# A hybrid decoder step: two small products of the cached attention get the full 128x128 shape, and the memory scores of a block stand in one place

## The reference, cut to what matters

```python
def mem_attend(q, mem_k, mem_v):                       # prompt: 256 memory tokens, 4 heads of width 64
    s = jnp.einsum('bshd,bmhd->bhsm', qh, mem_k).astype(jnp.float32) * (HEAD_DIM ** -0.5)
    pr = jax.nn.softmax(s, axis=-1).astype(q.dtype)
    return jnp.einsum('bhsm,bmhd->bshd', pr, mem_v).reshape(B, S, MEM_W)

def attend(q_lat, q_rope, ckv_new, krope_new):         # sample: one token against its paged cache
    s_past = jnp.einsum('bqhr,bkr->bhqk', q_lat, ckv_past) + jnp.einsum('bqhd,bkd->bhqk', q_rope, krope_past)
    ...
    pr = jax.nn.softmax(s, axis=-1).astype(ckv_new.dtype)
```

## Time and profile before

| | |
|---|---|
| median of 3 runs | 3482.54 us |
| span of the profiled execution | 3478.6 us |
| time outside the span, against the median | 3.9 us |
| TensorE busy | 3399.5 us (98%) |
| TensorE on the chain that ended last | 88% |
| VectorE, ScalarE, GpSimd busy | 58%, 36%, 7% |
| mean granted TensorE clock | 0.997 |
| TensorE idle before L827, for ScalarE's `Sm` | 4.5 us, 12 times |

### The profile page before, as it was taken

One profiled execution on the slowest core, in us unless ns is written; L12 is line 12 of the kernel. 1 busy time (PEld: TensorE's weight loads), 2 busy tenths in 40 slices (PEclk: granted clock), 3 DMA queues, 4 the chain that ended last, 5 costly groups with the idle time before them and its releaser, 6 DMA issues.

```text
span 3478.6 us, 80470 instructions
## 1 busy us (share of the span) xinstructions
PE 3399.5 (98%) x33076; PEld 2589.1 (74%) x33076; DVE 2030.8 (58%) x5212; ACT 1264.2 (36%) x3599; POOL 243.5 (7%) x284
## 2 busy tenths in 40 slices
PE   7999999999999999999999999999999999999998
PEld 6778686877869778686567787869777687776864
DVE  4656565665656556565346566666656565564653
ACT  2333334242343423524433233333423435234343
POOL 4100100000010000000041001000000000000000
PEclk9999999999999999999999999999999999999999
DMA  8654453626336163252366635436173351732512
GB/s 234 206 175 151 158 178 119 204 75 201 130 115 208 52 211 120 106 186 70 111 200 190 206 125 179 157 126 208 52 236 119 124 176 50 244 104 96 192 56 69
DMA packets 281024, 514.82 MB, mean 148 GB/s; under 512 B 30037, under 2 KB 215571, under 8 KB 268115
## 3 DMA queue, kind: packets, MB, share of 16 engines
q1 hardware_dynamic: 258903, 463.96, 40.7%
q0 software_dynamic: 11648, 41.95, 3.5%
q10 hardware_dynamic: 10108, 3.76, 0.4%
HBM read 473.15 MB, written 47.49 MB: 150 GB/s over the span
## 4 chain that ended last, share of the span: by engine, by line
PE 88%; ACT 4%; DVE 3%; issue 2%; DMA 2%; DVEq 1%; POOL 0%; ACTq 0%; POOLq 0%; SPq 0%
PE bank L823 81%; PE bank L827 7%; DMA win<-in_w_in 1%; DVEq L1555 1%; DMA wout<-in_w_out 1%; ACT Q L2603 1%; ACT PT L2718 1%; ACT qr L2602 0%; DVE mix L1785 0%; ACT Sm L2673 0%; ACT Q L2601 0%; DVE swaa L1783 0%; DVE mix L1781 0%; ACT hT L2426 0%; ACT PT L2523 0%
## 5 line engine op out<-in xcount | busy, mean ns | idle before, releaser
L823 PE MATMUL bank<-hT,win 128*128 128x256 f32 (+3 forms) x6384 | 1190.7, 339 | 6.5 <-DMA win<-in_w_in 3.3
L823 PEld LDWEIGHTS bank<-hT,win 128*128 128x128 f32 (+1 forms) x6384 | 951.1, 186 | 145.0 <-issue 33.4
L823 PE MATMUL bank<-wout,win 128*128 128x128 f32 x3136 | 379.9, 276 | 0.0
L823 PEld LDWEIGHTS bank<-wout,win 128*128 128x128 f32 x3136 | 364.6, 192 | 1.0
L823 PE MATMUL bank<-kv,Q 96*128 96x512 f32 (+3 forms) x640 | 276.4, 529 | 0.2
L1922 DVE TENSOR_REDUCE ml<-bank 128x1 f32<-128x512 f32 (+3 forms) x320 | 195.2, 610 | 124.5 <-PE bank L823 114.1
L827 PEld LDWEIGHTS bank<-cst,Sm 128*128 128x128 f32 x1344 | 157.5, 140 | 134.9 <-issue 72.0
L2673 ACT ACTIVATE Sm<-bank,ml 128x512 f32<-128x512 f32 (+3 forms) x320 | 199.8, 625 | 76.8 <-DVE ml L1927 70.0
L827 PE MATMUL bank<-cst,Sm 128*128 128x128 f32 x1344 | 210.7, 278 | 11.4 <-ACT PT L2523 5.9
L823 PE MATMUL bank<-wout,mix 128*128 128x512 f32 x480 | 215.1, 598 | 2.8 <-DMA wout<-in_w_out 1.7
L2449 ACT ACTIVATE mix<-bank 128x256 f32<-128x256 f32 x128 | 49.0, 383 | 333.1 <-PE bank L823 333.1
(11 more groups left out here) (527 smaller groups left out, 5955.9 us busy)
## 6 DMA issues: line engine op xcount, KB each, us to landing
win<-wfast SPq DMA_DIRECT2D x98, 1024.0 KB, 6.8
win<-in_w_in SPq DMA_DIRECT2D x78, 1024.0 KB, 5.7
win<-wfast SPq DMA_DIRECT2D x98, 768.0 KB, 6.2
wout<-in_w_out SPq DMA_DIRECT2D x60, 512.0 KB, 7.9
out_xres<-xin SPq DMA_DIRECT2D x16, 1024.0 KB
win<-in_w_in SPq DMA_DIRECT2D x16, 896.0 KB, 4.9
PT<-in_w_out SPq DMA_DIRECT2D x28, 512.0 KB, 4.4
XX<-in_w_out SPq DMA_DIRECT2D x28, 512.0 KB, 4.6
```

Of the source, the lines that this page charges most:

```text
L823: return pe.matmul(out, lhsT, rhs, start=start, stop=stop, skip_group_check=True)
```

## The change

The diagonal `dmx` gets 128 rows and the maxima `sd` 128 columns, both set to zero once. The transpose of slot 8 then takes all 128 columns, and the product of slot 9 contracts over 128 rows. VectorE still reads and writes 8 rows. The memory scores' group 0 moves from behind turn(n-4) to behind turn(n-2), directly ahead of group 1.

```diff
-        sd = sb("sd", [P, 72]); dmx = sb("dmx", [8, 16]); fin = sb("fin", [P, 48])
+        sd = sb("sd", [P, P]); dmx = sb("dmx", [P, 16]); fin = sb("fin", [P, 48])
...
                     if c + 5 < n:
                         scores(c + 5)
-                    if c in (n - 4, n - 2):
-                        memory_scores(B, (c - n + 4) // 2)
+                    if c == n - 2:
+                        memory_scores(B, 0)
+                        memory_scores(B, 1)
                     if c > m and (c - m) % 4 == 0:
...
                     pe.wait_ge(s_dm1.h, s_dm1.at(n, 1))
-                    tr(PP[7][0:8, 384:512], sd[:, 0:8], P).then_inc(s_dmt.h, 1)
+                    tr(PP[7][:, 384:512], sd[:, :], P).then_inc(s_dmt.h, 1)
                 elif slot == 9:
                     pe.wait_ge(s_dmd.h, s_dmd.at(n, 1))
-                    mm(PP[7][:, 400:408], ones[0:8, :], dmx[:, 0:8]).then_inc(s_dmb.h, 1)
+                    mm(PP[7][:, 400:408], ones, dmx[:, 0:8]).then_inc(s_dmb.h, 1)
...
-                v.tensor_reduce(dmx[:, 8:9], PP[7][0:8, 384:512], AX, MAX)
+                v.tensor_reduce(dmx[0:8, 8:9], PP[7][0:8, 384:512], AX, MAX)
                 drain()
-                v.tensor_scalar(dmx[:, 0:8], ident[0:8, 0:8], dmx[:, 8:9], None, MULT).then_inc(s_dmd.h, 1)
+                v.tensor_scalar(dmx[0:8, 0:8], ident[0:8, 0:8], dmx[0:8, 8:9], None, MULT).then_inc(s_dmd.h, 1)
...
             v.memset(dav4[:, :], 0.0)
+            v.memset(sd[:, :], 0.0)
+            v.memset(dmx[:, :], 0.0)
```

## The result

| | before | after |
|---|---|---|
| median | 3480.61 us | 3485.99 us |
| executions | 20 | 20 |
| span of the profiled execution | 3478.6 us | 3481.1 us |
| TensorE idle before L827 for ScalarE's `Sm` | 4.5 us, 12 times | 14.4 us, 24 times |

The changed kernel is slower by a ratio of 1.0016, with a 95% interval of 1.0009 to 1.0023: 5.6 us, between 3.1 and 8.0. The forecast was +5.0 us. One of the 20 executions after took 3876.64 us at a granted clock of 0.85 and is not in the ratio; without it the median is 3485.26 us.

What follows compares the result with a forecast made beforehand. TensorE, busy 98% of the span, and its waits for ScalarE in the attention tails were taken as the bound. -4.1 + 0.8 + 8.3 = +5.0 us, giving 3487.5 us, range 3481.5 to 3491.0 us.

Steps and rivals of the forecast that it cites:

- TensorE's order and its waits are the time: Whole kernel: TensorE is busy 98% of the span, so other engines count only where TensorE waits for them.
- Slot 9, 4.1 us gained: Product of `dmx`: full shape saves 0.29 us in 14 of 16 units, nothing at the layers' ends.
- Slot 8, 0.8 us lost: Transpose of `sd`: the full load costs 0.06 us more than the narrow one in 14 units.
- most of a load hides: Slot 8's transpose: rows taken to support the direction, not the size, of the page's 0.10 us more per unit.
- Group 0 covered a wait for ScalarE: Attention tails: moving the group leaves TensorE waiting for exponentials; with the joined group's price, 8.3 us lost over both layers.
- The joined group, 0.87 us for the second half: Memory scores behind turn(n-2): a group joined to another costs four pairs of passes at 0.22 us each.
- Nothing late further down, and no absorption: Behind the tails: VectorE's later maxima, about 0.8 us, delay nothing, and later TensorE waits do not shrink.
- TensorE is the bound in the tails too: Rival, attention tails: every change of shape saved is a gain, -8.3 us to 3474.2 us; chance 8%.
- Slot 9 gives nothing: Rival, product of `dmx`: its cost is its own latency, not shape; whole +9.1 us, 3491.6 us; chance 10%.
- The lost cover is given back: Rival, later in the blocks: TensorE's waits shrink by half or more of 8.3 us, about 3483 us; chance 12%.
- a fifth of 70%: Share of the forecast's own chance given to a kernel slower by over 0.2%, above 3489.5 us; written as 12%.
- The signs: Profile after: `Sm` waits over 10 us, gaps in 12 of 16 blocks, joined group about 2.0 us, 1.03 us over `dmx`.

Runs made afterwards that it cites:

- e1_small_only: The changed kernel with the memory scores back where they stood before, so only the two small products are in full shape; 3474.24 us, ratio 0.9985.
- e2_memory_only: The kernel before with only the memory scores joined behind turn(n-2), small products as before; 3489.91 us, ratio 1.0033 against the kernel before.
- e7_twice: The changed kernel with an extra copy of memory-score group 0 behind turn(n-4), signalling nothing to other engines; one execution, 3496.81 us.
- e3_alternate: The changed kernel with the loops of a memory group swapped, so products alternate between upper and lower row half; 3482.66 us, ratio 1.0011 against the kernel before.
- e4_dmx_only: The changed kernel with memory scores where they stood before and slot 8's transpose narrow again, only slot 9's product full; one execution, 3474.07 us.

## Why the prediction was right

- *TensorE's order and its waits are the time.* Right: the distances by place add up to +6.6 us, and each part alone gives its share of it (`e1_small_only`, `e2_memory_only`).
- *Slot 9, 4.1 us gained.* Right: 0.28 to 0.29 us in each of 14 units, 4.0 us, and nothing in the two at the layers' ends, as forecast. The neighbour of full shape was a good measure.
- *Slot 8, 0.8 us lost.* Right: 4.0 us without the wide transpose and 3.2 with it. One reading beside it was wrong: that most of a load hides. The load grew from 83 to 138 ns, and these 55 ns stand whole in the distance to the next pass; it is the estimate of 0.10 us from the count of columns that was too large.
- *Group 0 covered a wait for ScalarE.* Right in place and in kind; `e7_twice` shows it block by block. The forecast that the turns of blocks 2, 4 and 5 would not come forward held to 0.01 us.
- *The joined group, 0.87 us for the second half.* Too little. It is 0.96 us, since behind the joint the row halves fall out of step. That is the mis-sized term, 16 x 0.09 = 1.4 us of the sum (9.8 against 8.3), and `e3_alternate` removes it, 1.7 us. I took the step between pairs from inside a single group, where no load for a second group stands in line.
- *Nothing late further down, and no absorption.* Right: from `cxs,cst` to the memory values the sum over 16 blocks differs by 0.01 us.
- *The rivals.* "TensorE is the bound in the tails too" (-8.3 us) falls with the wait of 1.14 us at turn(n-3). "Slot 9 gives nothing" falls with `e1_small_only`. "The lost cover is given back" falls with `e2_memory_only`. In the chances behind them, a fifth of 70% is 14%, not 12%.
- *The signs.* All came: 14.4 us of waits for `Sm`, new or longer waits at turn(n-3) or turn(n-2) in blocks 2 to 7 of both layers (12 of 16), 2.10 us for the joined group, and 1.04 us over `dmx`.

The Trainium skill says in "TensorEngine Tiling (Array Packing)", section "Key Properties", that changing the tiling mode drains TensorE. The trace agrees that a change of shape costs time, though no row shows the drain itself: without the changes slot 9 is 0.28 us shorter per product, and the two blocks of m = 0, which had nothing covered, are 0.11 us shorter each. In the other blocks this was outweighed.

The forecast of 3487.5 us stood on the median of 3482.5 us of three runs; over 20 the kernel before has 3480.6, so the difference of +5.0 is what compares, with 5.6 (3.1 to 8.0) measured and 6.6 by the distances. The executions cannot tell 5.0 from 6.6; that the medians came nearer to the forecast than the distances did is luck. In 3487.5 against the 3485.99 measured, a base that was 1.9 us too high stood against a loss that was forecast too small.

## What to carry to other kernels

A product that costs a change of shape may still be free if it stands where its engine waits anyway; before such pieces are put together, read when the next instruction's operand is ready, place by place, since here the same move was worth -0.11 us in one block and +0.96 in another. Padding a tiny product to the full shape paid where its neighbours have that shape (0.28 us) and gave nothing where they have another; what it is worth can be read beforehand from a full-shape product nearby. Where products work on two row halves side by side and groups of them follow each other, try issuing the halves by turns: here it won 0.10 us per joined group.

## What the runs showed of the hardware

- A 64*128 group issued as upper, upper, lower, lower ran in step by itself, pairs 0.22 us apart, but not when a second group followed directly: from the sixth pair on single passes started 0.11 us apart, 0.10 us lost per joined group. Issued by turns it stayed in step (`e3_alternate`).
- A transpose of 8 columns that writes partitions 0 to 7 went over into full passes as one of full shape does: the next pass started 0.11 us after it (`e4_dmx_only`), where leaving a product of 8 rows took 0.18 us. Its load took 83 ns, padded to 128 columns 138 ns, and the next pass came 0.06 us later.
- A product of two passes in 8*128 shape among 128*128 passes cost 0.28 us more than in full shape; among 128*8 passes the two cost the same, 0.31 and 0.32 us to the next pass.
- The granted clock of the same unchanged stretch (1726 to 1912 us) was 0.96 in one profiled execution and 0.99 in another, and the stretch was 2.5 us shorter, nearly half of the effect that was to be measured. Some of this is waits that differed too.
